# Modulation as columns and as broadcast rows on the chip, without a trip through DRAM, in a long two-block kernel

## The chip, the cores and the metric

One core of one Trainium2 chip. The metric is the device time of one execution in microseconds, the median of several runs. Everything is float32; the large matrix products use a split of each operand into a high and a low fp32r half and three products of them, and the small ones plain f32.

## The reference, cut to what matters

256 tokens of width 1024 go through two layers of a first block and two of a second. Only the first block has the modulation, a vector of 6 x 1024 numbers for each layer:

```python
c_act = jax.nn.silu(c)                                   # (1, 1024)
for layer in range(2):
    mod = c_act @ mod_w[layer] + mod_b[layer]            # (1, 6144)
    sh_m, sc_m, gt_m, sh_f, sc_f, gt_f = jnp.split(mod[:, None, :], 6, axis=-1)
    h = x * (1 + sc_m) + sh_m
    u, q, k, v, g_out, a_low = jnp.split(h @ w_in[layer], IN_SPLITS, axis=-1)
    y = concat([s5(u), gla(q, k, v, g_out, a_low)]) @ w_out[layer]
    x = layer_norm(ALPHA * x + (1 + gt_m) * y, ...)
    h = x * (1 + sc_f) + sh_f
    f = swiglu(h) if layer % 2 == 0 else moe(h)
    x = layer_norm(ALPHA * x + (1 + gt_f) * f, ...)
```

Shifts and scales (sh, sc) are used with features on partitions, so the kernel wants them as columns (128 partitions, 8 numbers each). The gates (gt) multiply a result with tokens on partitions, so they are wanted as rows that stand on all 128 partitions.

## The kernel before

Each engine has its own program, written as strands (generators) that a function `weave` runs piece by piece in the order of a string in `ORDERS`, one string for each stage and engine. A letter is one piece; a piece reaches to the next `yield`. An engine executes strictly in that order, so a piece that waits holds up all behind it. Between stages stands a `fence` of all engines. SP issues all large weight loads in one order, 1 MB each (128 partitions x 2048), into a ring of five slots `RG`; a slot is loaded again when its user has said so (`W.raw_used` for those used as they are).

`mod_w` has 12 blocks of 512 columns for each layer, two loads each. `plan_mod` plans blocks 0 to 3 of layer 0 (shift and scale of the mixers) ahead of `w_in`, blocks 4 to 11 in the mixers of layer 0, and blocks 6 to 9 of layer 1 in the mixers of layer 1. What layer 1 needs otherwise comes from sums made beside the feed-forward; these don't change here, apart from the row sums' place in the order.

- `pe_mod`: one column of c (`sm(24 + k, 1)`, 128x1) is the stationary operand, 512 columns of the weight stream past it; 8 matmuls for a block give one row on one partition, in bank 3. The trace shows each f32 matmul as two records.
- `a_mod`: ACT copies the row (1x512) to SBUF and issues its DMA to `mod_rows` in DRAM. The next block waits for the copy.
- `a_cols`, `pe_cols`, `v_cols`: when all rows are in DRAM, a DMA reads them back with 128 numbers in a line, TensorE transposes them, and VectorE adds the bias `MB` and 1.
- `a_gate`, `v_gate`: the gates of layer 0 are read back from DRAM onto all partitions, the bias beside them into `ROWT`; VectorE adds both and 1 (128x1024, twice for each gate). Both gates share `ROWT`.

The strands of the stage "start" are `p` (`pe_first`, `v_first`, `a_first`: small transposes of biases and gains, the four blocks, the columns, then the scaled and transposed input `h_mod` in four quarters and the projection `w_in` in 17 parts) and `r` (the S5 coefficients: row arithmetic on 32 partitions, their transposes to `PC`, the input matrices in four rounds `v_s5_in`, then jobs B, C and K on TensorE, each emptied by ACT or VectorE). The stages "mixers0" and "mixers1" have strands `s` (S5: products of 32 rows and 64 columns, a long block of VectorE operations on 128x1024 with two scans, then products back), `g` (gated linear attention: decay, key transposes and the copy of keys `KD`, states, six levels of decayed queries and keys, scores, outputs), `m` (`pe_mods`, `v_mods`, `a_mods`) and `b` (VectorE: S5 weights of layer 1; ACT: loads for later). Small loads go out on ACT's queue, each as an instruction of its own in ACT's order.

Of the kernel before, what the change touches and what calls it, by code (L numbers as in the profile page):

```python
# [8 lines left out]
F32 = mybir.dt.float32  # L9
# [325 lines left out]
def weave(eng, stage, **strands):  # L335
# [37 lines left out]
def build(nc, w):  # L373
    ctx = ExitStack()
    with ctx:
# [44 lines left out]
        mrow = nc.dram_tensor("mod_rows", (2, 6144), F32, kind="Internal").ap()  # L420
# [35 lines left out]
        ROWT = ROWS[:, 2560:3584]  # L456
        g2 = lambda n, l: w[n + "_2"][l]
# [93 lines left out]
        c_in, first_in = signal("c_in", by=16), signal("first_in", by=16)  # L551
        silu_v, silu_a = signal("silu_v"), signal("silu_a")
        mod_pe, mod_a = signal("mod_row_pe"), signal("mod_row_a")
        row_sent = [signal(f"mod_row_sent{i}", by=16) for i in range(4)]
        cols_in, cols_pe, cols_v = signal("mod_cols_in", by=16), signal("mod_cols_pe"), signal("mod_cols_v")
        gate_in, gate_v = signal("gate_rows_in", by=16), signal("gate_rows_v")
# [7 lines left out]
        def mod_index(l, n):  # L564
            return n if l == 0 else 6 + n

        def pe_mod(pe, l, n):
            i = mod_index(l, n)
            pe.wait_ge(silu_v, 0, "c")
            pe.wait_ge(mod_a, i)  # L570
            pe.wait_ge(cols_v, (i >= 4) + (i >= 12))
            for ld in W.of["mod", l, n]:
                if ld.g:
                    yield
                pe.wait_ge(W.landed[ld.slot], ld.use)
                for k in range(4):
                    x = pe.mm(PS[0:1, 3, :], sm(24 + ld.g + k, 1), ld.dst[:, k, :], ld.g + k == 0, ld.g + k == 7)
                x.then_inc(W.raw_used)
            yield

        def a_mod(a, l, n):
            i = mod_index(l, n)
            ld = W.of["mod", l, n][1]
            row = ROWT[0:1, n % 2 * 512:(n % 2 + 1) * 512] if l else MOD[0:1, (n % 4) * 512:(n % 4 + 1) * 512]
            a.wait_ge(*ld.raw)
            if l == 0:
                a.wait_ge(row_sent[n % 4], i // 4)
            elif n >= 8:
                a.wait_ge(row_sent[(n - 2) % 4], 4)
            a.act(row, PS[0:1, 3, :], ACT.Copy).then_inc(mod_a)  # L590
            a.dma(mrow[l:l + 1, n * 512:(n + 1) * 512], row).then_inc(row_sent[n % 4])


        COLS = ((0, 0, 4, 4), (0, 6, 10, 12), (1, 6, 10, 16))

        def a_cols(a, k):
            l, n0, n1, sent = COLS[k]
            for r in range(4):
                a.wait_ge(row_sent[r], sent // 4)
            if k:  # L600
                a.wait_ge(cols_pe, k)
# [18 lines left out]
        def a_gate(a, i, dst):  # L620
            k = int(i == 5)
            for r in range(4):
                a.wait_ge(row_sent[r], 3)
# [2687 lines left out]
```

## Time and profile before

| | us |
|---|---|
| three runs | 2982.76, 2988.92, 2990.46 (median 2988.92) |
| the execution that was profiled | 2986.9 |
| its span, first to last instruction | 2985.1 |
| TensorE busy | 2556.5 (86%) |
| VectorE busy | 2058.9 (69%) |
| ScalarE busy | 1566.1 (52%) |
| mean granted TensorE clock | 0.905 of 2.4 GHz |

The stages follow each other by fences: the start to 133 us, the mixers of layer 0 to 289, output and feed-forward to 634, the projection of layer 1 to 694, its mixers to about 831, then the mixture of experts and the second block. In a timeline a line is one instruction or a run of like ones ("x16"), with start, length, and in brackets how long the engine had been idle before it and what released it. PE is TensorE, PEld its weight loads, DVE VectorE, ACT ScalarE; a q behind the name is the engine's queue of DMA issues or semaphore work. The length of a matmul record holds its way through the array, so the pace of a run is read from the starts. "fp32r" and f32 weights are both listed as f32.

### The profile page before, as it was taken

The numbers are of one execution on the slowest core, as the hardware profiler recorded it, in microseconds if no ns is written. First come the engines' busy times: TensorE is split into PE (matmuls) and PEld (weight loads), VectorE is DVE, ScalarE is ACT, GpSimd is POOL, SyncE is SP. The second block draws the span as 40 slices with busy tenths as digits, with TensorE's granted clock in tenths as the row PEclk, the third lists the DMA queues.
The fourth block names the chain that finished last, engine by engine and source line by source line (L and its number), as shares of the span: only waits on it lengthen the run. The fifth ranks groups of instructions, "written<-read, shape, count | busy, mean of one in ns | idle before, by whom it ended". The sixth has DMA issues, their size and how long they took to land.

```text
span 2985.1 us, 31552 instructions
## 1 busy us (share of the span) xinstructions
PE 2556.5 (86%) x11718; PEld 1997.7 (67%) x11718; DVE 2058.9 (69%) x2204; ACT 1566.1 (52%) x1938; POOL 24.4 (1%) x33
## 2 busy tenths in 40 slices
PE   5997789977967999999999999968686998786898
PEld 2736677855556777777777777756455786555787
DVE  5597786755666888887978888874664554565454
ACT  2222434432146878787787878753533544543443
POOL 0000000000100000000000000000000000000000
PEclk9987999986978999999999999988777999877899
DMA  8461367731335998898989898974012454303352
GB/s 254 129 195 38 108 215 263 272 114 49 111 116 195 328 330 326 310 349 303 345 320 355 327 333 331 339 258 142 23 57 85 156 188 145 113 24 104 100 186 96
DMA packets 274723, 599.15 MB, mean 201 GB/s; under 512 B 28801, under 2 KB 35311, under 8 KB 273409
## 3 DMA queue, kind: packets, MB, share of 16 engines
q1 hardware_dynamic: 252144, 580.30, 54.8%
q10 hardware_dynamic: 22418, 16.77, 2.1%
q8 instruction: 94, 1.54, 0.2%
q14 instruction: 67, 0.55, 0.1%
HBM read 595.93 MB, written 1.09 MB: 200 GB/s over the span
## 4 chain that ended last, share of the span: by engine, by line
PE 61%; DVE 23%; ACT 10%; issue 2%; ACTq 1%; DMA 1%; DVEq 0%; POOL 0%; POOLq 0%; PEldq 0%
PE PS L205 59%; DVE WL L167 8%; ACT WH L197 3%; PE PS L213 2%; ACT AR L197 2%; DVE AR L167 2%; DVE MW L167 2%; ACTq L146 1%; DVE WF L167 1%; ACT MW L197 1%; DVE HF L167 1%; DVE MOD L167 1%; ACT L197 1%; ACT WF L197 1%; DVE HTR L167 1%
## 5 line engine op out<-in xcount | busy, mean ns | idle before, releaser
L167 DVE TENSOR_TENSOR WL<-RG,WH 128x1024 fp32r<-128x1024 f32 (+1 forms) x558 | 919.4, 1648 | 446.7 <-ACT WH L197 417.6
L197 ACT ACTIVATE WH<-RG 128x1024 fp32r<-128x1024 f32 x782 | 827.4, 1058 | 594.1 <-PE PS L205 527.6
L205 PE MATMUL PS<-WH,HTR 128*128 128x512 f32 (+3 forms) x2920 | 926.2, 393 | 63.2 <-DVE HTR L167 21.9
L205 PEld LDWEIGHTS PS<-WH,HTR 128*128 128x128 f32 x2920 | 557.7, 194 | 197.7 <-DVE WL L167 40.4
L205 PE MATMUL PS<-WL,HTR 128*128 128x512 f32 (+3 forms) x1460 | 569.1, 390 | 0.0
L205 PE MATMUL PS<-WH,ATR 128*128 128x512 f32 x1624 | 522.5, 395 | 16.6 <-DVE WL L167 9.3
L205 PEld LDWEIGHTS PS<-WH,ATR 128*128 128x128 f32 x1624 | 309.2, 190 | 85.0 <-DVE WL L167 19.1
L205 PE MATMUL PS<-MW,HTR 128*128 128x512 f32 x1332 | 330.0, 397 | 18.1 <-DVE MW L167 18.1
L205 PE MATMUL PS<-WL,ATR 128*128 128x512 f32 x812 | 319.8, 394 | 0.0
L205 PEld LDWEIGHTS PS<-WL,HTR 128*128 128x128 f32 x1460 | 282.7, 194 | 52.5
L167 DVE TENSOR_TENSOR MW<-RG,MW 128x2048 fp32r<-128x2048 f32 x112 | 256.7, 2292 | 64.1 <-ACT MW L197 53.4
L205 PEld LDWEIGHTS PS<-MW,HTR 128*128 128x128 f32 x1332 | 248.3, 190 | 70.7 <-DVE MW L167 20.3
L197 ACT ACTIVATE MW<-RG 128x1024 fp32r<-128x1024 f32 x224 | 237.9, 1062 | 25.2 <-PE PS L205 2.5
L205 PEld LDWEIGHTS PS<-WL,ATR 128*128 128x128 f32 x812 | 154.8, 191 | 31.5
L213 PE MATMUL PS<-KC,AR 128*128 128x128 f32 (+2 forms) x716 | 118.1, 301 | 63.0 <-DVE AR L167 24.3
L213 PEld LDWEIGHTS PS<-KC,AR 128*128 128x128 f32 (+2 forms) x716 | 94.2, 156 | 90.0 <-DVE AR L167 30.8
L205 PE MATMUL PS<-RG,SMALL 128*1 128x512 f32 x256 | 121.2, 625 | 9.1 <-ACT ROWS L197 5.2
L197 ACT ACTIVATE AR<-PS,SMALL 128x128 f32<-128x128 f32 (+3 forms) x146 | 77.5, 531 | 75.8 <-PE PS L205 67.9
L197 ACT ACTIVATE AR<-PS 128x512 f32<-128x512 f32 (+3 forms) x120 | 66.7, 556 | 82.2 <-PE PS L205 50.0
L213 PE MATMUL PS<-KC,X 128*128 128x128 f32 x160 | 33.8, 393 | 81.1 <-ACTq L155 31.1
L197 ACT ACTIVATE ATR<-PS 128x512 fp32r<-128x512 f32 x102 | 61.1, 599 | 80.3 <-PE PS L213 75.4
L213 PEld LDWEIGHTS PS<-KC,X 128*128 128x128 f32 x160 | 29.3, 207 | 85.5 <-DVEq L155 37.3
(219 smaller groups left out, 2037.7 us busy)
## 6 DMA issues: line engine op xcount, KB each, us to landing
RG<-in_moe_w_gate SPq DMA_DIRECT2D x112, 1024.0 KB, 5.7
RG<-in_moe_w_up SPq DMA_DIRECT2D x112, 1024.0 KB, 5.8
RG<-in_moe_w_down SPq DMA_DIRECT2D x112, 1024.0 KB, 6.2
RG<-in_w_ff SPq DMA_DIRECT2D x64, 1024.0 KB, 5.2
RG<-in_mod_w SPq DMA_DIRECT2D x48, 1024.0 KB, 5.3
RG<-in_w_in SPq DMA_DIRECT2D x36, 1024.0 KB, 5.2
RG<-in_w_out SPq DMA_DIRECT2D x16, 1024.0 KB, 5.0
RG<-in_ffn_w_gate SPq DMA_DIRECT2D x14, 1024.0 KB, 5.2
```

The source lines that it names most:

```text
L146: return Ins(self.e.dma_start(dst, src, **kw) if self.e is not None else None, self)
L167: return self.did(lambda: self.e.tensor_tensor(o, a, b, op))
L197: return self.did(lambda: self.e.activation(o, a, f, bias=bias, scale=scale))
L205: return self.did(lambda: self.e.matmul(o, l, r, start=start, stop=stop))
L213: return self.did(lambda: self.e.transpose(o, a, perm))
```

## The change

The row on one partition, its copy to DRAM and its reading back are gone. Blocks that are needed as columns (0 to 3 and 6 to 9) hold 128x128 pieces of the weight as the stationary operand and stream one column of c past them: 16 matmuls of one column for a load, 128 for the eight loads of four blocks, into 32 columns of bank 3 (16 for each half of the sum); VectorE adds the two halves and the bias. Blocks that are needed as rows (4, 5, 10, 11 of layer 0) hold c on all 128 columns (`CBC`, 8 pieces of 128x128 made once by VectorE in `ROWT`), so that the result stands on all partitions; VectorE adds it and 1 to the bias, which has been loaded into the gate's place. ACT has no part in it any more. TensorE waits for the constants as its first act. The loads for S5 (`a_s5_in(a, 0)`) are issued after ACT's row pieces and no more before the first stage; the small transposes of biases come after the four blocks. The orders of the start and of both mixers are others.

```diff
 ORDERS = {
-    ("mixers0", "a"): "gmsbmsbgmgsggmmmmmggggggmsmmsggggsgggsmssggg",
+    ("mixers0", "a"): "gsbmsbggsggsgggsgggsgggssggsggggg",
-    ("mixers0", "pe"): "mmggsmmsmmmmsmmgsmmgmggmggmsmssggssssggsssggsssggsssgsmssssggggggggg",
-    ("mixers0", "v"): "bggsbgsgbgsmgssssgbbggbggbggbgggggggggsggggggsgggggmgmsggmggsggssgggggg",
+    ("mixers0", "pe"): "mmmgmsmgsmmmmmmmmgsssssssgmggssssgsgmsssssssggsmggsggsggmgsggggggggg",
+    ("mixers0", "v"): "mgsbmbgsmggbgsssssgbgbgmgggbggsgggggggsgmbgsgbgggggmggsgggsgsgggggggggggg",
-    ("mixers1", "a"): "sgmbssggggsgggsgggsgggbggmgsgssmmggmmg",
+    ("mixers1", "a"): "gsmbbgssgggsggggggsgggggggssssggg",
-    ("mixers1", "pe"): "sggsmmgsssgsgsggsgsmssssssssssssggmsggmsgmgggsgmsmggmgmgggmggmgmm",
-    ("mixers1", "v"): "gsbmsgggsgggssssggmgggggggggggmgssgmsgmggggggggggsgssgggggggggggmg",
+    ("mixers1", "pe"): "ggsmmmsmgsssgmggsmsggmsmssssggssssgssgsggsggsgmmssggmggmgssgggmgm",
+    ("mixers1", "v"): "bgsmgggsmgmsggssssggmggmggggggggggsggsgggggggggggsggggggsgssggmggg",
-    ("start", "a"): "rprrrpppprrrprppprprrrpppppppppppppppppppppp",
-    ("start", "pe"): "ppprpppprpprrrrrppppprrrrrrrrrpppppppppppppppppp",
-    ("start", "v"): "rpprrrrrrrrrrrrprrprprpprpprppprrppppppppppppppppppppp",
+    ("start", "a"): "rprrrrpprrrpprrrpppppprrpppppppppppppppp",
+    ("start", "pe"): "prppppprpppprrrrrpppprppprrppppppppppprrprrprprp",
+    ("start", "v"): "rprrrrrrrrrrrppppppppppprpprrppppppppppppppppprrrrrprp",
...
+        CBC = ROWT.rearrange("p (k n) -> p k n", k=8)
...
+        MODS = (0, 0, 4), (0, 4, 1), (0, 5, 1), (0, 6, 4), (0, 10, 1), (0, 11, 1), (1, 6, 4)
+
+        def pe_mod(pe, i):
+            l, n0, m = MODS[i]
             pe.wait_ge(silu_v, 0, "c")
+            for n in range(n0, n0 + m):
+                for ld in W.of["mod", l, n]:
+                    yield
+                    if n == n0 and ld.g == 0:
+                        pe.wait_ge(mod_v, i)
+                    pe.wait_ge(W.landed[ld.slot], ld.use)
+                    if m == 1:
+                        for k in range(4):
+                            x = pe.mm(PS[:, 3, :], CBC[:, ld.g + k, :], ld.dst[:, k, :], ld.g + k == 0, ld.g + k == 7)
+                    else:
+                        for j in range(4):
+                            c = ld.g * 4 + (n - n0) * 4 + j
+                            for k in range(4):
+                                x = pe.mm(PS[:, 3, c:c + 1], ld.dst[:, k, j * 128:(j + 1) * 128], sm(24 + ld.g + k, 1),
+                                          k == 0, k == 3)
+                    x.then_inc(W.raw_used)
+
+        def v_mod(v, i):
+            l, n0, m = MODS[i]
+            v.wait_ge(*W.of["mod", l, n0 + m - 1][1].raw)
+            if m == 1:
+                dst = (GTM if n0 < 6 else GTF)[:, n0 % 2 * 512:n0 % 2 * 512 + 512]
+                v.wait_ge(gate_in, 2)
+                v.stt(dst, PS[:, 3, :], 1.0, dst, ADD, ADD).then_inc(mod_v)
+                return
+            a_ = 48 * l + 4 * n0
+            v.tt(MC[:, a_:a_ + 16], PS[:, 3, 0:16], MB[:, a_:a_ + 16], ADD)
+            v.tt(MC[:, a_:a_ + 16], MC[:, a_:a_ + 16], PS[:, 3, 16:32], ADD).then_inc(mod_v)
+            v.ts(MC[:, a_ + 8:a_ + 16], MC[:, a_ + 8:a_ + 16], 1.0, None, ADD)
+
+        def a_gate_bias(a):
+            for i, dst in ((2, GTM), (5, GTF)):
+                a.dma(dst, rowb(w["mod_b"][0, i * 1024:(i + 1) * 1024])).then_inc(gate_in)
...
         def pe_first(pe):
-            yield
-            pe.wait_ge(first_in, 7)
+            yield from pe_mod(pe, 0)
+            yield
+            pe.wait_ge(first_in, 6)
             pe.tr(PS[:, 7, 0:96], CB[0:96, 128:256], KC[0:96, K_ID:K_ID + 96])
             pe.tr(PS[:, 7, 96:144], CB[0:48, 256:384], KC[0:48, K_ID:K_ID + 48]).then_inc(pro_pe)
-            for n in range(4):
-                yield from pe_mod(pe, 0, n)
-            pe_cols(pe, 0)
             yield
             pe.wait_ge(pro_v, 1)
+            pe.wait_ge(mod_v, 1)
             yield from pe_w_in(pe, 0)
...
         def a_s5_first(a):
             yield from a_s5_rows(a)
+            yield
+            a_s5_in(a, 0)
             yield from a_s5_jobs(a, 0, S5_BANKS[0], JOBS)
 
         def pe_program(pe):
+            pe.wait_ge(consts_in, 1)
...
             v.tt(sm(24, 8), CB[:, 0:8], sm(16, 8), MUL).then_inc(silu_v, "c")
+            v.wait_ge(consts_in, 1)
+            for k in range(8):
+                v.ts(CBC[:, k, :], KC[:, K_ONE:K_ONE + 128], sm(24 + k, 1), None, MUL)
```

## Rows read from the trace of the kernel before

**Rows 1.** The page, chain that ended last, shares by engine.
```profile
PE 61%; DVE 23%; ACT 10%; issue 2%; ACTq 1%; DMA 1%; DVEq 0%; POOL 0%; POOLq 0%; PEldq 0%
```

**Rows 2.** Windows: stretch, length, busy PE, PEld, DVE, ACT, POOL, clock, DMA, GB/s.
```profile
82.00:133.00 51.00, 50.85 (x240) 43.19 (x239) 23.11 (x29) 16.20 (x19) 0.00 (x0) 0.96 0.39 125
133.00:289.00 156.00, 132.58 (x703) 72.80 (x703) 131.28 (x202) 32.23 (x50) 8.87 (x12) 0.80 0.40 125
694.00:835.00 141.00, 102.72 (x656) 63.63 (x656) 92.83 (x140) 33.06 (x49) 9.35 (x12) 0.77 0.21 68
755.00:822.00 67.00, 60.07 (x276) 30.79 (x275) 43.23 (x59) 9.91 (x19) 5.49 (x7) 0.97 0.39 127
```

**Rows 3.** Timeline of the start: start, length, engine, operation, count, idle before.
```profile
19.50 8.57 PE L205 MATMUL PS<-RG,SMALL 128*1 128x512 f32 x16
...
29.54 7.03 PE L205 MATMUL PS<-RG,SMALL 128*1 128x512 f32 x16 [1.47 <-ACT MOD L197]
...
46.12 0.43 DVE L167 TENSOR_TENSOR MOD<-MOD,PC 128x256 f32<-128x256 f32 x1
...
50.32 0.42 DVE L167 TENSOR_TENSOR MOD<-MOD,PC 128x256 f32<-128x256 f32 x1
...
53.03 0.22 ACTq L146 DMA_DIRECT2D mod_rows<-MOD  x1
...
71.12 10.31 PE L205 MATMUL PS<-AR 128*128 128x128 f32 x64 [2.15 <-DVE AR L171]
...
75.70 2.36 DVE L172 TENSOR_SCALAR H<-PS,SMALL 128x256 f32<-128x256 f32 x4
...
81.74 0.50 PE L205 MATMUL PS<-WH,HTR 128*128 128x512 f32 x1
```

**Rows 4.** Timeline, TensorE, feed-forward of layer 0: one-column products.
```profile
502.10 3.63 PE L205 MATMUL PS<-SMALL,H 128*128 128x1 f32 x32
```

**Rows 5.** Windows, columns as in group 2: narrow blocks.
```profile
128.40:133.00 4.60, 4.45 (x22) 4.36 (x21) 0.11 (x1) 0.11 (x1) 0.00 (x0) 0.51 0.00 0
502.00:505.60 3.60, 3.60 (x35) 3.56 (x33) 1.23 (x1) 1.06 (x1) 0.00 (x0) 1.00 0.25 100
```

**Rows 6.** Timeline, TensorE, last block of the first projection: 16 columns.
```profile
125.76 0.26 PE L205 MATMUL PS<-WL,HTR 128*128 128x16 f32 x1
...
126.10 0.26 PE L205 MATMUL PS<-WL,HTR 128*128 128x16 f32 x1
...
129.72 0.36 PE L205 MATMUL PS<-WL,HTR 128*128 128x16 f32 x1
...
130.36 0.36 PE L205 MATMUL PS<-WL,HTR 128*128 128x16 f32 x1
```

**Rows 7.** Timeline, mixers of layer 0: TensorE, then VectorE.
```profile
154.95 13.24 PE L205 MATMUL PS<-H,AR 32*128 32x64 f32 x256 [1.75 <-DVE H L181]
...
171.26 2.47 DVE L167 TENSOR_TENSOR HF<-AR,PS 128x1024 f32<-128x1024 f32 x2
...
191.07 0.69 DVE L167 TENSOR_TENSOR WF<-WF 128x512 f32<-128x512 f32 x1
...
200.36 0.69 DVE L181 COPY WF<-PS 128x512 f32<-128x512 f32 x1
...
214.35 10.10 DVE L167 TENSOR_TENSOR WF<-WF 128x128 f32<-128x128 f32 x18
...
263.47 1.22 DVE L167 TENSOR_TENSOR MOD<-MOD,ROWS 128x1024 f32<-128x1024 f32 x1 [0.93 <-DMA ROWS<-in_mod_b]
```

**Rows 8.** Timeline, mixers of layer 1: ACT, VectorE, TensorE.
```profile
786.33 0.95 ACT L197 ACTIVATE WF<-WF 128x256 f32<-128x256 f32 x2 [6.38 <-issue]
...
786.78 4.28 DVE L167 TENSOR_TENSOR WF<-WF 128x256 f32<-128x256 f32 x7 [4.12 <-ACT WF L197]
...
788.01 4.88 PE L205 MATMUL PS<-RG,SMALL 128*1 128x512 f32 x8 [5.19 <-ACT ROWS L197]
...
828.44 0.28 PE L213 MATMUL PS<-KC,ST 16*128 16x16 f32 x1 [6.76 <-DMA ST<-mod_rows]
```

More of the change, by code:

```diff
@@ L360 @@
     ("attention1", "v"): "kbccddddbbcbccdckddkbcdbcdbccddccbdbdcdcbcdbcccdbdddddcbcddcdbcbckkk",
-    ("start", "a"): "rprrrpppprrrprppprprrrpppppppppppppppppppppp",
-    ("start", "pe"): "ppprpppprpprrrrrppppprrrrrrrrrpppppppppppppppppp",
-    ("start", "v"): "rpprrrrrrrrrrrrprrprprpprpprppprrppppppppppppppppppppp",
+    ("start", "a"): "rprrrrpprrrpprrrpppppprrpppppppppppppppp",
+    ("start", "pe"): "prppppprpppprrrrrpppprppprrppppppppppprrprprrprp",
+    ("start", "v"): "rprrrrrrrrrrrppppppppppprpprrppppppppppppppppprrrrrprp",
     ("out0", "a"): "xxrrwwrxxrrwwwrrwxrrxxwwwwwxwxwwwxxxxxxxx",
@@ L549, in build @@
         oown = {x: signal("over_own_" + x) for x in ("v", "a", "g")}
-        c_in, first_in = signal("c_in", by=16), signal("first_in", by=16)
+        c_in, consts_in, first_in = signal("c_in", by=16), signal("consts_in", by=16), signal("first_in", by=16)
         silu_v, silu_a = signal("silu_v"), signal("silu_a")
[L553 to L556, printed above, removed]
+        mod_v, gate_in = signal("mod_v"), signal("gate_bias_in", by=16)
         rows_in = signal("rows_in", by=16)
@@ L574, in pe_mod @@
                     yield
[L575 to L578, printed above, removed]
-            yield
[L581 to L591, printed above, removed]
@@ L594, in build @@
[L594 to L601, printed above, removed]
-            m = 4 * (n1 - n0)
-            a.dma(ST[0:m, 384:512], mrow[l, n0 * 512:n1 * 512].rearrange("(j p) -> j p", p=128)).then_inc(cols_in)
-        def pe_cols(pe, k):
-            l, n0, n1, sent = COLS[k]
-            m = 4 * (n1 - n0)
-            pe.wait_ge(cols_in, k + 1)
-            pe.wait_ge(mod_a, sent)
-            pe.tr(PS[:, 3, 0:m], ST[0:m, 384:512], KC[0:m, K_ID:K_ID + m]).then_inc(cols_pe)
@@ L612, in v_cols @@
-        def v_cols(v, k):
-            l, n0, n1, sent = COLS[k]
-            a_, b_ = 48 * l + 4 * n0, 48 * l + 4 * n1
-            v.wait_ge(cols_pe, k + 1)
-            v.tt(MC[:, a_:b_], PS[:, 3, 0:b_ - a_], MB[:, a_:b_], ADD)
-            c = 48 * l + 8 * (1 if n0 == 0 else 4)
-            v.ts(MC[:, c:c + 8], MC[:, c:c + 8], 1.0, None, ADD).then_inc(cols_v)
[L620 to L623, printed above, removed]
-            a.wait_ge(gate_v, k)
-            a.dma(dst, rowb(mrow[0, i * 1024:(i + 1) * 1024])).then_inc(gate_in)
-            a.dma(ROWT, rowb(w["mod_b"][0, i * 1024:(i + 1) * 1024])).then_inc(gate_in)
@@ L1456, in pe_mods @@
                 pe.wait_ge(sums_v, 0, "row3")
-            for n in (range(6, 10) if l else range(4, 12)):
-                yield from pe_mod(pe, l, n)
-            pe_cols(pe, 1 + l)
+                yield from pe_mod(pe, 6)
+            else:
+                for i in range(1, 6):
+                    yield from pe_mod(pe, i)
         def v_mods(v, l):
@@ L1463, in v_mods @@
                 yield from v_row_sums(v)
-            yield
-            v_cols(v, 1 + l)
-            v_ln_cols(v, l, 8 * l, 16 + 8 * l, 4)
-            if l == 0:
+            for i in ((6,) if l else range(1, 6)):
                 yield
-                v_gate(v, 2, GTM)
-                yield
-                v_gate(v, 5, GTF)
-        def a_mods(a, l):
-            for n in (range(6, 10) if l else range(4, 12)):
-                yield
-                a_mod(a, l, n)
-            yield
-            a_cols(a, 1 + l)
-            if l == 0:
-                yield
-                a_gate(a, 2, GTM)
-                yield
-                a_gate(a, 5, GTF)
+                v_mod(v, i)
+                if i in (3, 6):
+                    v_ln_cols(v, l, 8 * l, 16 + 8 * l, 4)
         def nothing(*_):
@@ L1503, in a_mixers @@
         def a_mixers(a, l):
-            weave(a, f"mixers{l}", s=a_s5(a, l), g=a_gla(a, l), m=a_mods(a, l),
+            weave(a, f"mixers{l}", s=a_s5(a, l), g=a_gla(a, l), m=iter(()),
                   b=once(lambda: (a_second_in(a), a_ln_rows(a, 1, "mix", 1))) if l else once(lambda: a_s5_in(a, 1)))
@@ L3054, in a_first @@
         def a_first(a):
-            for n in range(4):
-                yield
-                a_mod(a, 0, n)
-            yield
-            a_cols(a, 0)
             for _ in range(4):
```

20 lines of the change are left out of this document (3 added, 17 removed).

## The prediction

> **What bounds the kernel now.** I read the shares of the chain first, then the busy time by stage, then the timelines of the three stages that the change touches. TensorE has most of the chain, VectorE the next share [rows 1]. The change works in the start (0 to 133 us), in the mixers of layer 0 (133 to 289) and of layer 1 (694 to 835). The projection inside the start keeps TensorE busy for all of its 51 us; in the first mixers VectorE (131 of 156 us) and TensorE (133) are both nearly full; in the second TensorE has 103 and VectorE 93 of 141 [rows 2]. So in the start and late in both mixers a TensorE microsecond is a microsecond of the kernel; under the long VectorE block of the recurrence it is free.
>
> In the start TensorE does nothing until 19.5 us, because its first piece waits for the last small load; then come four row products (first records at 19.50, a later group 7.03 us for 16 records), the last row leaves for DRAM at 53.03, the scaled input is formed at 75.70, and the projection starts at 81.74 [rows 3].
>
> **Cost of the new product.** Before, one 1 MB load is 4 matmuls of 512 columns, 8 records. As columns it is 16 matmuls of one column, each behind a 128x128 f32 weight load, 32 records. The trace holds this very shape once: 32 records in 3.63 us, the last start 3.4 us behind the first, so 0.108 us a record and 3.45 us a load at the 2.4 GHz level [rows 4]; its window shows a granted clock of 1.00 [rows 5]. That equals the row form (half of 7.03, [rows 3]): at full clock the change of form is free.
>
> At the lower level it isn't. The last block of the projection is the nearest long run of narrow matmuls: 16 columns, weights of 128 columns loaded back to back. It begins at full clock with 3 records in 0.34 us; some 3 us later 3 records take 0.64 us, 0.213 each [rows 6], and the window shows 0.51 although TensorE is busy for 4.45 of 4.60 us [rows 5]. So a TensorE that loads weights all the time and streams next to no columns falls to 1.2 GHz, and a weight-load-bound record doubles. One column is further that way than 16. The burst of [rows 4] lasted 3.6 us between wide matmuls and says nothing of 28 us. Ends for one load: 3.45 us and 32 x 0.213 = 6.8 us. I take 6.8 for the runs of eight loads, since the 16-column row is the nearest long one, and a value between for scattered loads. The Trainium skill (page "TensorE: Matmul & The Clock Gate", LDWEIGHTS) prices a weight load at its columns over 1.2 GHz, with no word of the granted clock. By it the load would stay near 3.4 us; the rows at 0.110 and 0.213 us disagree.
>
> **Start.** Removed: four ACT copies, four writes to DRAM, the read back, one transpose, and the wait of the first product for the small loads. Added: a wait for the constants (issued first) and eight 128x128 VectorE operations, about 2 us before VectorE's first row piece, which waits for its own loads anyway: 0. Gate bias loads and the S5 loads move on ACT's queue; they end well before their users: 0 to +1, as the first scaled copy stands behind seven issues instead of five.
> - TensorE starts at about 9 us, an estimate: it needs c and the first MB, which is moved beside the constants; the first window of the trace has no row for either. Five loads at 6.8: 43. Row transposes 2: 45. Three loads: 65.5. Small transposes 1, five S5 jobs at 0.9 to 1.7: 74.
> - VectorE: PC copy, then three rounds of the S5 input at 4.2 us (46.12 to 50.32 [rows 3]): 59, no bound. Bias and modulation: 67. Then four low halves, the last held by ACT's S5 copies and high halves: 76, then scaling, which took 6.0 us to the first matmul (75.70 to 81.74): 82 to 83. So the projection starts 1 us later than before, though the DRAM trip is gone.
> - The new order also puts S5 jobs inside the projection: three B jobs, two C jobs (5 x 0.87, from 8 records at 0.108) and the four K jobs, before at 71.12 in 10.31 us, partly at low clock [rows 3], at 0.108 for 64 records 6.9. That is 11 us on a TensorE that has none free there.
> Sum +12. At full clock: five loads end by 29, VectorE's rows at 32 and its three rounds bind instead (51), projection at 62, plus 62: 124, so -9.
>
> **Mixers of layer 0.** Two row loads, two more, then S5's 32-row products (13.24 us, [rows 7]), as before. Then TensorE has eight column loads in one string, the key transposes behind them. From the stage start: 34 + 8 x 6.8 = 88.5, transposes to 90. VectorE does its block (19.8 us from 171.26 to 191.07), two S5 rounds, and wants the keys at about 65; before it got them at 200.36, 67.4 us into the stage [rows 7]. It stands idle until 90: +22.5. Behind that the order has seven S5 pieces, the state products and a row load before VectorE's levels, which before began at 214.35, 81.3 us in; now about 109, as the pieces were under the wait before: +28. Off come two gate pieces on VectorE (1.2 + 0.7 each) and a wait of 0.93 for a DMA [rows 7]; on come four adds of 128x512 (0.7, as the copy of that size) and one S5 round that has moved late: 0. Sum +28. At full clock the string ends at 62, under VectorE's 65, and the stage gains 2.
>
> **Mixers of layer 1.** Gains: the read back through DRAM at the end (TensorE waited 6.76 us; about 4 of it are on the path, because ACT's table load and VectorE's last product stand behind it), and ACT's 13 issues in mid-stage, for which VectorE stood 4.12 us and TensorE 5.19 [rows 8]. These issues now come as ACT's first work of the stage, 6.3 us, ahead of the gate's exponentials and the copy that S5's products wait for: +4. Column loads are scattered among 31 us of other TensorE work (60 busy from 755 to 822, [rows 2], less 29 for the loads). If all eight ran at the low level it would be +27, none 0; I take half, 13, because each load alone is as short as the burst that kept its clock, while pairs aren't. Sum 13 + 4 - 4 - 4 = +9; bounds -4 and +23. ACT's eleven other row copies were never late: 0.
>
> **Sum.** 12 + 28 + 9 = +49 us on the execution that was profiled, 2986.9 (span 2985.1), which is 2.0 below the median 2988.92: 3036. Weights for the later stages use the same ring of five slots, and their stages are untouched: 0.
>
> **Rivals.**
> 1. *Weight loads keep their pace* (clock stays at 2.4 GHz, or the load doesn't follow it). For: the one-column burst held 1.00 [rows 5]. Against: the 16-column run. Then start -9, first mixers -2, second -4: 2972, faster.
> 2. *The low clock comes, but where TensorE has room.* For: the second block of idle TensorE under the recurrence is some 20 us long. Against: in the start and in the first mixers the string is longer than its cover. If the string in the first mixers cost only 5, and the second mixers nothing: 2986.9 + 12 + 5 - 1 = 3003; with a start at 0 it is 2991.
> 3. *The low clock spreads*: full-duty work behind each scattered load also starts low, as TensorE does after the row 128.40 to 133 [rows 5]; second mixers at +23, start at +20: 3058.
> 4. *The change doesn't do what it says*, the DRAM trip was hidden anyway: the start and the tail of the second mixers gain nothing even at full clock. Then the moved S5 jobs alone count, between 0 and +11: 2990 to 3000. It decides only if rival 1's clock holds.
>
> Rival 1 takes over where a column load costs less than about 4.4 us: each microsecond above 3.45 is worth 6 in the start (21 over 3.35) and 4 in the second mixers, and 8 in the first mixers from 3.8 us on, where their string outgrows its cover; with these, -15 becomes 0 at 4.4.
>
> **How the numbers follow.** Forecast with its own spread (3015 to 3050) 0.55; rival 3 0.15; rival 1 0.18; rivals 2 and 4 together 0.12. The time is that of the likeliest, 3036. The range leaves out little of the first two and reaches down to rival 1: 2970 to 3060, 0.9 of the chance less the tails, some 0.8; the likeliest's own is 3015 to 3050. A measurement of this kernel tells about 0.3%, 9 us, from no change. Faster by more: 0.19 (rival 1 and a little of 4). Within: 0.06. Slower: 0.75.
>
> **What the new profile would show.** Right: records of one column 0.213 us apart over nearly all of 9 to 65 us, granted clock 0.5 there; in the first mixers a string of 256 such records over 54 us and VectorE idle over 20 us before the key copy; projection beginning at 82 and lasting 62. Wrong: one-column records at 0.108 us through a whole string, or a projection that begins before 70. The step most open is the clock under one-column products longer than 3.6 us; the second is how many of the scattered loads fall low. If TensorE starts later than 12 us, the loads and not the clock bind the start.

## The result, and the profile after

The changed kernel takes 3061.8 us (median; 3057.5 to 3082.8), the kernel before 2989.4 in the same session: ratio 1.026 (95% interval 1.023 to 1.028), some 72 us slower. The profiled execution took 3063.1 us, 3061.3 of it span. The forecast was 3036, its range ended at 3060.

I cut both traces at the same five events: the projection's first matmul, ScalarE's copy of its last 16 columns, the first matmul that waits for GpSimd at the end of the first mixers, the same copy in layer 1, and the same matmul at the end of the second mixers. Each stage is the time between two of them, in us, one profiled execution each (a difference of two rounded times can be off by 0.1):

```
                         before    after   difference   forecast
start to projection        81.7     81.1      -0.6         +1
projection                 51.2     61.0      +9.9        +11
mixers of layer 0         156.2    185.4     +29.2        +28
middle of the layer       405.1    409.6      +4.5          0
mixers of layer 1         137.6    169.9     +32.3         +9
rest                     2153.3   2154.2      +0.9          0
span                     2985.1   3061.3     +76.2        +49
```

The timeline of the changed kernel, TensorE in the start and in the first mixers, then VectorE's copy of the keys (start, length, engine, line, operation, count, idle before it and what ended that), to be read against [rows 3] and [rows 7]:

```profile
9.80 34.27 PE L205 MATMUL PS<-SMALL,RG 128*128 128x1 f32 x160 [9.80 <-DMA RG<-in_mod_w]
...
45.41 20.64 PE L205 MATMUL PS<-SMALL,RG 128*128 128x1 f32 x96
...
176.35 54.77 PE L205 MATMUL PS<-SMALL,RG 128*128 128x1 f32 x256
...
232.11 0.69 DVE L181 COPY WF<-PS 128x512 f32<-128x512 f32 x1 [22.12 <-PE PS L213]
```

The records are 0.214 us apart from 9.8 to 66 us (34.27 over 160) and again for 54.77 us in the first mixers, where one short burst in the kernel before had 0.113 [rows 4]. VectorE stands idle for 22.12 us before the keys. It copies them 89.9 us into the stage, 22.4 later than before; the forecast had 90 and 22.5. Windows of the changed kernel (stretch, length, busy PE, PEld, DVE, ACT, POOL, clock, DMA, GB/s), against [rows 2] and [rows 5]:

```profile
8.00:66.00 58.00, 56.20 (x269) 56.15 (x269) 31.01 (x90) 4.52 (x7) 0.00 (x0) 1.00 0.75 235
176.00:231.00 55.00, 55.00 (x265) 54.88 (x262) 31.75 (x43) 5.97 (x7) 0.00 (x0) 0.50 0.42 134
737.00:907.00 170.00, 142.90 (x839) 126.68 (x839) 91.78 (x139) 27.62 (x42) 8.88 (x12) 0.58 0.18 57
```

The string of the first mixers runs at the lower level (0.50 is 1.2 GHz) although TensorE is busy for 55.00 of 55.00 us. The clock was at that level before the string began, at 165 us, under S5's 32-row products; it didn't come back until the string was over. In the start the clock column says 1.00 at the very same pace of records; there the pace is what counts (last section).

In the second mixers nearly all loads ran low, and so did much of what stands between them. TensorE there, late in the stage:

```profile
847.06 3.35 PE L205 MATMUL PS<-WF 64*128 64x128 f32 x14
850.34 6.98 PE L205 MATMUL PS<-SMALL,RG 128*128 128x1 f32 x32
857.25 3.35 PE L205 MATMUL PS<-WF 64*128 64x128 f32 x14
860.53 0.79 PE L205 MATMUL PS<-AR,WF 128*128 128x128 f32 x2
861.26 0.79 PE L205 MATMUL PS<-WF 64*128 64x128 f32 x2
861.98 6.98 PE L205 MATMUL PS<-SMALL,RG 128*128 128x1 f32 x32
```

Six loads take 6.98 or 6.99 us each. The two that stand together (from 831.38) take 11.32, because they begin at full clock and lose it on the way (last section). The same fourteen score matmuls (64 rows, 128 columns) that take 1.82 us at full clock take 3.35. The windows from 845 to 890 us, between and under the loads alike, show 0.50 and a TensorE without a gap:

```profile
845.00:860.00 15.00, 15.00 (x67) 14.46 (x67) 4.03 (x5) 0.22 (x1) 0.00 (x0) 0.50 0.25 80
860.00:875.00 15.00, 15.00 (x64) 14.01 (x64) 5.57 (x6) 0.00 (x0) 0.00 (x0) 0.50 0.33 120
875.00:890.00 15.00, 15.00 (x64) 13.87 (x63) 5.68 (x8) 1.86 (x3) 0.00 (x0) 0.50 0.00 0
```

In the kernel before, the window from 755 to 822 us had 0.97 [rows 2].

### The profile page after: what moved, and what is told of

Same layout as the page of the kernel before. It is cut to its first block, busy times and chain, and to the rows that moved or that the text cites. A ratio compares the mean times of both kernels' runs of the same rounds, so it can differ in the third digit from the quotient of the medians.

```text
span 3061.3 us, 32653 instructions
## 1 busy us (share of the span) xinstructions
PE 2654.5 (87%) x12291; PEld 2174.0 (71%) x12291; DVE 2059.2 (67%) x2215; ACT 1556.7 (51%) x1922; POOL 24.0 (1%) x33
## 4 chain that ended last, share of the span: by engine, by line
PE 66%; DVE 20%; ACT 9%; issue 2%; DMA 1%; ACTq 1%; DVEq 0%; POOL 0%; SPq 0%; POOLq 0%; PEldq 0%
PE PS L205 63%; DVE WL L167 7%; PE PS L213 3%; ACT WH L197 3%; ACT AR L197 2%; DVE MW L167 2%; DVE AR L167 1%; ACT MW L197 1%; DVE MOD L167 1%; ACT L197 1%; DVE HTR L167 1%; DVE WF L167 1%; ACT WF L197 1%; DVE H L167 1%; DVE X L167 1%
## 5 line engine op out<-in xcount | busy, mean ns | idle before, releaser
L205 PE MATMUL PS<-SMALL,RG 128*128 128x1 f32 x768 | 162.9, 349 | 9.8 <-DMA RG<-in_mod_w 9.8
L205 PEld LDWEIGHTS PS<-SMALL,RG 128*128 128x128 f32 x768 | 162.1, 328 | 12.0 <-issue 11.6
L213 PE MATMUL PS<-KC,X 128*128 128x128 f32 x160 | 32.5, 387 | 80.3 <-ACTq L155 30.6
```

The lines of the kernel that those rows point to most:

```text
L205: return self.did(lambda: self.e.matmul(o, l, r, start=start, stop=stop))
L213: return self.did(lambda: self.e.transpose(o, a, perm))
```

## The experiments

**The theory.** A long run of one-column products pulls TensorE to 1.2 GHz or holds it there, and the whole loss comes from that. Rivals: the column form itself costs it at any clock; the new orders and waits cost it; ScalarE's small-load issues at the head of the second mixers cost 4 us, as the prediction had it.

**1. The same products, 128 equal columns wide.** The moving operand is the same column of c read 128 times. Other widths weren't tried. Weight loads, order and waits stay; only what TensorE streams behind each load grows. The last product to write a column of PSUM is the one meant for it, and the second half of the sum lies from column 256 on, where VectorE reads it.

```
-c = ld.g * 4 + (n - n0) * 4 + j
+c = ld.g * 64 + (n - n0) * 4 + j
-x = pe.mm(PS[:, 3, c:c + 1], ld.dst[:, k, ...], sm(24 + ld.g + k, 1), ...)
+x = pe.mm(PS[:, 3, c:c + 128], ld.dst[:, k, ...], sm(24 + ld.g + k, 1).broadcast_to([128, 128]), ...)
```

> Changed kernel, but every column product streams 128 equal columns of c instead of one (same weight loads, same number of matmuls; one of the 128 result columns is used). Clock theory: the one-column strings are slow because TensorE falls to 1.2 GHz; with 128 columns it stays at 2.4 and a record takes 0.108 us instead of 0.213. Then the start is some 9 us shorter than in the kernel before (projection from about 62 us), the mixers of layer 0 about 154 us long instead of 185, those of layer 1 about 134 to 140 instead of 170: near 2970 us in all, faster than the kernel before. Shape theory (a one-column product with weights from the ring costs 0.21 us whatever the clock; more columns can't make it cheaper): stays at 3060 or above. Order theory (the new orders cost most of it): records at 0.108 but stages still long, 3020 to 3050.

Measured: 2992.2 us, ratio to the kernel before 1.001 (0.9997 to 1.002). So 70 of the 72 us go, with as many instructions as in the changed kernel and 128 times the columns. TensorE's timeline, start and first mixers:

```profile
9.69 20.69 PE L206 MATMUL PS<-SMALL,RG 128*128 128x128 f32 x160 [9.69 <-DMA RG<-in_mod_w]
...
168.18 30.72 PE L206 MATMUL PS<-SMALL,RG 128*128 128x128 f32 x256
```

The first string takes 20.69 us instead of 34.27, the second 30.72 instead of 54.77. Windows inside the second string, its first records and the rest:

```profile
168.10:172.00 3.90, 3.90 (x22) 3.83 (x19) 3.21 (x7) 3.78 (x4) 0.00 (x0) 0.50 0.00 0
173.00:199.00 26.00, 26.00 (x235) 26.00 (x235) 24.80 (x30) 0.85 (x2) 0.00 (x0) 1.00 0.84 270
```

This is the plainest evidence for the clock: one string of equal products, 0.213 us a record while the window shows 0.50 and 0.112 us while it shows 1.00. The string begins at the lower level, as in the changed kernel; with 128 columns the clock rises inside it, with one it never did. The window over the second mixers, against 0.58 and 142.90 busy above:

```profile
704.00:838.00 134.00, 107.70 (x843) 91.57 (x843) 91.93 (x139) 27.87 (x43) 8.88 (x12) 0.75 0.23 72
```

That stage takes 133.2 us, 36.7 less than in the changed kernel. TensorE's busy time shrinks by 35.2. Grouped by operation over the stage (count | busy us, mean ns | idle), the changed kernel first:

```profile
L205 PE MATMUL PS<-SMALL,RG 128*128 128x1 f32 x256 | 53.2, 343 | 0.0
L205 PE MATMUL PS<-WF 64*128 64x128 f32 x136 | 26.8, 359 | 0.0
```

and with 128 columns:

```profile
L206 PE MATMUL PS<-SMALL,RG 128*128 128x128 f32 x256 | 32.0, 284 | 0.0
L206 PE MATMUL PS<-WF 64*128 64x128 f32 x136 | 19.1, 283 | 0.3 <-DVE WF L168 0.3
```

The column products themselves account for 21.2 us of the 35.2, the scores for 7.7 and the other short matmuls for 6.3: two fifths of the loss in this stage lie in work that the change doesn't touch. The form rival falls. So does the order rival as the main cause, since the orders are the changed kernel's; what they cost by themselves stands below, under the mixers of layer 0.

The time was expected near 2970 us and is 22 above. The first mixers took 158.9 us (154 expected) and the middle 411.5 (405.1 before). The largest miss is the start: the projection began at 72.9 us, not at 62. VectorE's and ScalarE's timelines show why:

```profile
16.91 6.54 ACTq L147 DMA_DIRECT2D MOD<-in_s_b_im  x1
23.48 12.51 ACTq L147 DMA_DIRECT2D MOD<-in_s_c_re  x1
...
48.40 0.42 DVE L168 TENSOR_TENSOR MOD<-MOD,PC 128x256 f32<-128x256 f32 x1 [14.75 <-DMA SMALL<-in_s_b_glu]
```

The change moved the S5 loads behind ScalarE's exponentials. ScalarE is at issuing them until 40.94, and VectorE waits 14.75 us for the last. In the changed kernel VectorE stood 13.13 us for the row transposes behind the slow string instead, which hid this.

**2. ScalarE's issues later in the second mixers.** They are 15; the prediction and the expectation call them 13, the rows of the timeline, two of which are pairs. On top of the last kernel:

```
-("mixers1", "a"): "gsmbbgssgggsggggggsgggggggssssggg"
+("mixers1", "a"): "gsmbgssgggbsggggggsgggggggssssggg"
```

> As wide128, and ACT's 13 small-load issues of the mixers of layer 1 put behind the last exponential ahead of VectorE's long block, where ACT idled for some 30 us in the changed kernel, instead of first in the stage. If they delay the copy that S5's products wait for, as I reckoned at +4, this is 4 to 6 us faster than wide128; if the path there went by TensorE or VectorE anyway, the same.

Measured: 2994.1 us, ratio to the kernel before 1.001 (0.9997 to 1.002); the stage took 132.9 instead of 133.2 us. The issues cost nothing where the change put them.

**3. 128 columns in the second mixers alone.** The width is 128 for layer 1 and 1 elsewhere.

> The changed kernel with 128 equal columns in the eight loads of the second layer alone; those of the start and of the first layer keep their one column. Theory (each stage loses by its own low clock, and nothing carries over): start 142 us and the first mixers 185 us as in the changed kernel, the second mixers 133 us as in the wide one instead of 169.9, so 3022 to 3028 us. Rival (the clock lost in the first layer is paid in the second too, or a change of the order there is part of the loss): the second mixers at 140 to 165 us, 3030 to 3055 us.

Measured: 3028.0 us, ratio 1.012 (1.009 to 1.015). Start 142.3 and first mixers 182.8 us, near the changed kernel's 142.2 and 185.4; second mixers 136.9. The stage is 33 us shorter than in the changed kernel, about half of the 70 us that the clock costs in all, and the start and the first mixers keep their own loss. The 136.9 lies between the 133 of the theory and the 140 of the rival, but run 6, whose code is run 1's in this stage, read 136.7 there, so it is within the spread of the stage. Stages don't pay for each other, as far as that spread tells.

**4. The eight loads of the second mixers in one string, one column wide.**

```
-("mixers1", "pe"): "ggsmmmsmgsssgmggsmsggmsmssssggssssgssgsggsggsgmmssggmggmgssgggmgm"
+("mixers1", "pe"): "ggsmmmsmgsssgmggsmsggsssssggssssgssgsggsggsgmmmmmmmmssgggggssgggg"
```

> The changed kernel, one column as it has it, with the eight loads' products of the second layer together in one string instead of scattered in six places over the stage. Theory (a scattered piece pulls its neighbours down: of the 36 us that the low clock costs in this stage, some 21 lie in the column products themselves and some 14 in the short matmuls between them): the string runs low as a whole, 52 to 56 us for 256 records, but the others get the full clock back, and the stage takes 156 to 163 us instead of 169.9, so 3048 to 3055 us. Rival (all of the loss goes with the column products, wherever they stand): the stage stays at 168 to 172 us and the time at 3060 to 3064. Third case (the string waits for its loads, or keeps the others waiting, and this costs more than the clock gives back): over 172 us.

Measured: 3077.9 us, ratio 1.029 (1.027 to 1.032): the stage took 186.6 us, 16.7 more than scattered. The first expectation is refuted. TensorE around and behind the string:

```profile
820.97 0.71 PE L205 MATMUL PS<-WF 64*128 64x128 f32 x4
821.61 51.95 PE L205 MATMUL PS<-SMALL,RG 128*128 128x1 f32 x256
873.49 1.96 PE L205 MATMUL PS<-KC,HF 63*128 63x63 f32 x8
875.38 2.61 PE L205 MATMUL PS<-H,MOD 128*128 128x256 f32 x8
877.92 3.35 PE L205 MATMUL PS<-WF 64*128 64x128 f32 x14
```

and the window behind it, where nothing of one column is left:

```profile
875.00:915.00 40.00, 28.63 (x111) 25.23 (x110) 21.20 (x33) 5.83 (x8) 0.00 (x0) 0.50 0.07 26
```

A window inside the string shows the fall without a gap in TensorE's work:

```profile
822.00:870.00 48.00, 48.00 (x238) 48.00 (x239) 7.95 (x14) 2.82 (x7) 4.54 (x6) 0.53 0.44 144
```

TensorE enters the string fast, comes out at 1.2 GHz and stays there to the end of the stage, with the ordinary short matmuls alone.

**5. The same one string, 128 columns wide**, as the control for run 4.

> The order with one string in the second mixers, with 128 equal columns: the control for that run, where the stage took 186.6 us. Theory (the string lost its time by the clock: TensorE came out of it at half clock and stayed there to the end of the stage): 133 to 139 us in this stage, as in the scattered order with 128 columns. Rival (the order itself costs it, the other work waits behind the string): 148 to 155 us, some 17 above the scattered order, as in the narrow pair (186.6 against 169.9).

Measured: one execution, 3016.7 us; the stage took 157.9 us, 24.7 more than the scattered order at the same width. The rival is the nearer one: the order itself costs it, as the rest of the stage waits behind the string. TensorE:

```profile
791.91 28.85 PE L206 MATMUL PS<-SMALL,RG 128*128 128x128 f32 x256
...
823.07 1.82 PE L206 MATMUL PS<-WF 64*128 64x128 f32 x14
...
829.48 3.35 PE L206 MATMUL PS<-WF 64*128 64x128 f32 x14 [0.49 <-DVE MOD L168]
```

```profile
829.00:850.00 21.00, 17.63 (x68) 15.62 (x68) 10.44 (x12) 1.92 (x4) 0.00 (x0) 0.50 0.00 0
```

Here the string runs at full clock, and the same scores cost 1.82 us behind it, but 3.35 from 829 on: late in this stage TensorE falls to the lower level with no one-column product in it. So run 4 doesn't show that the narrow string alone holds the clock down to the end; between the two strings 28.7 us are the clock's, 23.1 of them in the string.

**6. The sums in the middle, widened too.** In the middle the kernel before already has sixteen one-column products (32 records). They took 3.63 us there [rows 4] and 4.78 in the changed kernel, and wide matmuls behind them ran slow.

```
-x = pe.mm(PS[:, 5, j:j + 1], HROW[:, j * 128:(j + 1) * 128], COL[:, 1:2], True, True)
+x = pe.mm(PS[:, 5, j:j + 128], HROW[:, j * 128:(j + 1) * 128], COL[:, 1:2].broadcast_to([128, 128]), True, True)
```

> The kernel with 128 equal columns, and the sixteen one-column sums in the middle of the layer (32 records) widened in the same way to 128 equal columns. Theory (the 3 to 4 us that the middle of the layer loses comes from the granted clock falling at this short string of one-column matmuls): the 32 records take 3.6 to 3.9 us instead of 4.67, the clock stays at 1.00 behind them, and the middle takes 407 to 409 us instead of 411.5, so 2988 to 2990 us. Rival (the middle is longer for another reason, and the short string only happens to lie there): the middle stays at 411 to 412 and the time at 2992 us.

Measured: 2990.0 us, ratio 0.999 (0.998 to 1.0005), against 1.001 without: the difference is inside the intervals. The stage took 406.8 us instead of 411.5, and the 32 records 3.73 us; the second mixers, unchanged in the code, took 136.7 instead of 133.2, so the whole shows little of it. The profiles of the other kernels agree: where the narrow burst took 3.63 us (before, before with early loads, run 4) the middle is 405.1 to 406.2 us long; in the seven others it took 4.65 to 4.87 and the middle 409.3 to 411.6. But both kernels without the change were on the short side, and seven of eight with it on the long one. Whether the change itself tips the burst or not was tried with a small shift: one or two more clears of a 128x1024 tile (0.91 us each) on VectorE at the head of this stage, in both kernels.

```
-for at in (HROW, GTM, ROWT):
+for at in (HROW, GTM, ROWT) + (GTM,):          # or + (GTM, GTM)
```

> The kernel before with one more clear of a 128x1024 tile on VectorE at the head of the feed-forward of layer 0, so that the sixteen one-column sums (32 records) come about 1 us later. Theory (these sums fall low or not by when they come, and the change only moved them in time): of the four shifted kernels some take 3.6 us for the records and some 4.6 to 4.9, in both families, and the middle is 405 to 407 us, or 409 to 412, with it, plus the shift of up to 1 us. Rival (something that the change does to the stage drops the clock there): both shifted kernels of the family before take 3.63 us and 405 to 407 us.

> The same with two more clears, about 2 us later. Same theories: a mixture over the four, or 3.63 us here and middle 405 to 408.

> The changed kernel with one more clear at the same place. Theory (time alone decides): a mixture over the four kernels, 3.6 or 4.6 to 4.9 us for the 32 records, middle 405 to 408 or 409 to 412. Rival (the change does it): 4.6 to 4.9 us and 409 to 412 here.

> The changed kernel with two more clears. Same theories as for one: a mixture over the four, or 4.6 to 4.9 us here.

Measured, one execution each: burst and middle in us are 3.63 and 408.4, then 3.81 and 411.9 for the kernel before with one and two clears, and 3.63 and 405.8, then 3.88 and 410.0 for the changed kernel. Windows from the start of the burst on, the kernel before with two clears first, then the changed kernel with one:

```profile
507.60:511.40 3.80, 3.80 (x34) 3.80 (x32) 1.23 (x1) 1.06 (x1) 0.00 (x0) 0.93 0.22 91
511.40:516.00 4.60, 4.60 (x16) 3.69 (x16) 0.00 (x0) 0.31 (x1) 0.00 (x0) 0.69 0.67 230
```

```profile
538.60:542.20 3.60, 3.60 (x34) 3.58 (x33) 1.23 (x1) 1.06 (x1) 0.00 (x0) 1.00 0.25 102
542.20:547.00 4.80, 4.80 (x22) 3.94 (x22) 0.73 (x1) 1.06 (x1) 0.00 (x0) 1.00 0.67 220
```

With a shift, the clock falls in the kernel before as well, and holds in the changed one, whose time (3052.7 us in that execution) is lower with a clear more than without. So both families know both outcomes, and the rival (something that the change does in the stage) falls.

What decides is open. The shifts weren't the ones intended: the burst begins 213.0 us into the stage in the kernel before and at 216.3 and 218.2 with one and two clears, but at 214.2 in the changed kernel and at 213.6 and 216.3 with them. And each kernel was profiled once, so that a difference between executions of one kernel isn't told from one between kernels. What the burst is worth is plainer when counted from its first record to the end of the stage: 192.1 or 192.2 us where the clock holds, 193.7 where it falls as the burst ends (both kernels with two clears, and run 4), and 195.3 to 196.8 where it falls inside the burst.

**7. The S5 loads of layer 0 from GpSimd's queue**, on top of the 128 columns. GpSimd has nothing to do in the start. Each of the four large loads is cut in two halves, on a semaphore of their own.

```
-            a_s5_in(a, 0)          # ScalarE, behind its exponentials
+            a_s5_in(g, 0)          # GpSimd, first of all
```

> The kernel with 128 equal columns, and the S5 loads of the first layer issued from GpSimd's queue, which is idle there, ahead of everything (each of the four large ones in two halves). In the wide kernel VectorE stands for 14.75 us, until 48.40, for the last of these loads, because ScalarE issues them from 16.47 to 40.94 us. Theory (the S5 loads' late issue on ScalarE is what holds the start): the wait is gone or under 3 us, the projection begins at 62 to 65 us instead of 73.0, everything behind moves up by as much, 2981 to 2984 us, some 6 to 9 us below the kernel before. Rival (the transfers themselves fill the DMA engines until about 48 us, whoever issues them): VectorE waits as long as before, projection at 71 to 75, 2990 to 2994 us.

Measured: 2985.4 us, ratio 0.997 (0.996 to 0.998). The projection begins at 65.4 us instead of 72.9.

```profile
40.89 0.43 DVE L168 TENSOR_TENSOR MOD<-MOD,PC 128x256 f32<-128x256 f32 x1 [6.71 <-DMA SMALL<-in_s_b_glu]
```

VectorE still waits 6.71 us, for the last small load. The issue was what held the start, though not all of it.

**8. The same edit in the changed kernel, one column wide, and in the kernel before.**

> The changed kernel with its one-column products, and the S5 loads from GpSimd's queue alone. Theory (with one column the start is bound by TensorE's string, which lasts until 66 us and hides ScalarE's issuing): the projection begins at 80 to 82 us as in the changed kernel, end of the start 141 to 143, so the S5 loads are worth 0 here, where they are worth 7.6 behind the wide products. Rival (they cost in both): projection at 73 to 77.

> The kernel before the change with the one edit that the S5 loads of the first layer are issued from GpSimd's queue. Theory (the start before the change is bound by the chain of four rows to DRAM and back, which the profile shows to end at 71.1 us, and the S5 loads lie beside it): projection still at 79 to 82, time 2987 to 2991 us, so the gain of 7 us needs the change's way without the trip. Rival (ScalarE's 14 us of issuing also holds the four rows' evictions, so the chain moves up with it): projection at 74 to 78, 2981 to 2985 us, and the change would be worth nothing in itself.

Measured: one execution of the changed kernel, 3063.6 us, projection at 82.1 and end of the start at 143.2 (142.2 without): no gain. The kernel before: 2991.2 us, ratio 0.999 (0.998 to 1.000), projection at 83.4 (81.7 without). Neither gains, as the theories had it (the projection of the second is 1.7 us later, which they hadn't). The late S5 loads cost nothing behind a slow string or behind the trip to DRAM, and 7.5 us behind fast products.

**9. The three edits together, then VectorE waiting for the B loads alone.** `best` joins 128 columns, wide sums and GpSimd's loads; `best2` adds to it:

```
-v.wait_ge(s5_soft_in, 10)     # all S5 loads, before the first block work
+v.wait_ge(s5_b_in, 4)         # B alone
+v.wait_ge(s5_c_in, 6)         # C, skip and gate bias: before the C matrix
```

> Three edits together on the changed kernel: 128 equal columns for the column products, the same for the sixteen sums in the middle of the layer, and the first layer's S5 loads from GpSimd's queue. Theory (the three gains lie in different stages and add): start 126.5 us to the end of the projection, first mixers 158.5, middle 405 to 407 instead of 409 to 411, second mixers 133 to 136, 2980 to 2983 us, ratio 0.996 to 0.998 to the kernel before. Rival (the middle's gain was the luck of one execution): 2985 us, as with the S5 loads alone.

> As the last, and VectorE's first block work waits for the B loads alone, on a semaphore of their own; the C loads, the skip and the gate bias are waited for only where the C matrix is formed. With the S5 loads on GpSimd, VectorE still stood 6.71 us, to 40.89, for the last small load, while GpSimd had issued the B halves by 24.9. Theory: that wait ends by 35 to 37, the projection begins at 60 to 62 instead of 65.4, and the time is 2976 to 2979 us. Rival (something else is the last before the projection: the w_in weights' conversion, X's transposes): the projection stays at 64 to 66 and the time at 2980 to 2983.

Measured: 2978.8 us, ratio 0.9955 (0.9943 to 0.9968), then 2970.8, ratio 0.9925 (0.9912 to 0.9938). Both intervals lie below 1, so both beat the kernel before. The first time lies just under its expectation, as it should if the gains of runs 6 and 7 add to run 1, though run 6's alone was inside its intervals. In the last, VectorE and TensorE:

```profile
32.97 0.56 DVE L182 COPY PC<-PS 128x384 f32<-128x384 f32 x1 [1.04 <-PE PS L214]
33.63 0.43 DVE L168 TENSOR_TENSOR MOD<-MOD,PC 128x256 f32<-128x256 f32 x1
...
59.70 0.79 PE L206 MATMUL PS<-WH,HTR 128*128 128x512 f32 x1 [9.88 <-DVE HTR L168]
```

There is no wait left between the two VectorE lines, and the projection begins at 59.7 us, 22 earlier than in the kernel before. By stage against the kernel before: start 120.9 (-12.0), first mixers 157.9 (+1.7), middle 405.6 (+0.5), second mixers 133.7 (-3.9), which is -13.7. The rest read 2147.6 us (-5.8); it is the same code in all kernels and read 2148.5 to 2156.2 in the sixteen other profiles, so most of that part looks like the spread of the stage. The time lies 5 us under the expected 2976; no run tells whether that is the spread too.

## Why the prediction failed, step by step

- **One-column products at half clock (right).** The weighing of the 16-column rows [rows 6] against the short burst [rows 4] came out as taken: 0.214 us a record, 6.8 to 7.0 us a load. Run 1 shows that it is the clock and not the load: with 128 columns behind every weight load, records are 0.213 us apart at 0.50 and 0.112 at 1.00, in one string. The Trainium skill (page "TensorE: Matmul & The Clock Gate", section LDWEIGHTS) prices a load by its columns alone, which makes 0.107 us for 128 of them, an estimate by that page. The records at full clock agree with it, those at the lower level are twice as far apart.
- **Start, +12 (right, +9.3).** The string began at 9.8 us (forecast about 9) and the projection at 81.1 (forecast 82 to 83), then lasted 61.0 (forecast 62).
- **S5 loads on ScalarE's queue at no cost (right by its number, wrong by its reason).** The text said that they end well before their users. They ended when VectorE was still held by TensorE's transposes (13.13 us). With fast products it waited 14.75 us for them. So rival 1's start was wrong too: 134.1 us, where it forecast 124. It would have missed by 10 us in this term.
- **Mixers of layer 0, +28 (right in the string, and in the sum by some luck, +29.2).** The string outgrew its cover as reckoned: the keys came 22.4 us later, forecast 22.5. The levels behind them began 105.6 us into the stage, 24.1 later than before, where 28 was forecast. The small terms behind them were put at 0. By the prediction's own prices they come to +2.3 (an S5 round of 4.2 and four adds of 0.7, less 4.7), and from the levels to its end the stage took 79.7 us instead of 74.8. Two errors of some 4 to 5 us cancel. The second is there at either width: the thirteen profiles with the new order have 77.0 to 80.3 us behind the levels, the four with the old 74.8 to 75.1. So at full clock (run 1) the levels began 2.8 us earlier than before and the stage was still 2.7 longer, where the prediction had a gain of 2. How the 2 to 5 us divide between the S5 round and two row loads that now stand there on TensorE (6.42 and 3.70 us in run 1) no run tells. Five other profiles with the same code in this stage read 182.3 to 182.9 us, so +29.2 is the upper end of +26 to +29.
- **Mixers of layer 1, +9 with bounds -4 and +23 (wrong, +32.3).** This is the step that failed, and with it the sum. It had three faults. First, it took half of the eight loads as low "because each load alone is as short as the burst that kept its clock"; all but the head of one pair were (six of 6.99 us, two in 11.32). The two at 795 and 803 us began at 0.50, and the pair lost the clock, with all behind it. Why these loads ran low where the burst kept its clock isn't shown. The surroundings differ: the burst stood between wide matmuls, these loads among short ones, which in run 5 ran low from 829 us on with no one-column product about. Secondly, its upper bound priced the loads alone. The neighbours lost 14.0 us more. Thirdly, its small terms were off but cancelled: ScalarE's issues at the head cost nothing clear of the spread (0.3 in run 2), not 4, and the two gains of 4 came to less than 5 together, as the stage is 4.4 us shorter than before at full clock. By the runs the term is +21.2 for the loads (13 was taken), +14.0 for their neighbours and +1.5 of idle time (none was), and -4.4, which is the +32.3.
- **Middle, 0 (wrong by size, +4.5).** The prediction called the middle untouched. The one-column burst there holds the full clock or loses it, in either family of kernels (run 6): from its first record on the stage is 3.3 us longer than before. The prediction had its row in hand [rows 4] and should have put these microseconds into the range. The other 1.3 us lie ahead of the burst and aren't traced.
- **Rivals.** Rival 3, the low clock that spreads to the work behind, named the mechanism of the failed term, at too small a size (+23 for that stage) and with a start of +20 that didn't come. Rival 1's ends show in run 1 for the second mixers (-4.4, it said -4). Against rival 4 speaks run 7 beside the kernel before with the same early loads: the start ends at 126.5 us instead of 135.3. So the start gains by the change at full clock. How much of it is the trip to DRAM and how much TensorE's earlier first product (11.1 instead of 22.1 us in these two) no run separates. In rival 2 the gain of 1 us in the second mixers has no source; by the prediction's own terms for that stage it would be 4. That makes 3000 of its 3003 and bears on no chance.

## What to carry to other kernels

A matmul with one moving column is not cheap because it streams little: price it at the lower clock, price the short matmuls around it at the lower clock too, and only then ask what hides it. In the stage that the prediction missed, the loads cost 21.2 us more and their neighbours 14.0. If its weight loads bind anyway, try the same products with equal columns added to the moving operand; here 128 of them, the one width tried, cost no instruction and gave 70 us back. When a slow step is made fast, look again at every transfer that it had hidden, since a cost that was called nothing is often only covered.

## What was not expected of the hardware

- TensorE busy for 55.00 of 55.00 us stayed at a granted clock of 0.50 (first mixers of the changed kernel), and the same 256 products with 128 columns took 30.72 us and rose to 1.00 within them. In run 4 the clock fell from 1.00 under one-column products, with TensorE busy for 48.00 of 48.00 us. The Trainium skill (page "TensorE: Matmul & The Clock Gate", "HAM oscillation — how this bites in real kernels") puts the fall of the clock down to idle gaps; the rows here have none.
- From a stretch at 1.00 (826 to 831 us in the changed kernel) the clock fell within two loads of one column:

```profile
831.40:833.50 2.10, 2.10 (x20) 2.10 (x20) 0.99 (x3) 1.43 (x3) 0.76 (x1) 1.00 0.01 4
835.00:838.00 3.00, 3.00 (x16) 3.00 (x15) 2.76 (x6) 0.54 (x2) 1.46 (x2) 0.50 0.30 33
```

- In the start the clock column reads 1.00 from 8 to 66 us while the records are 0.214 us apart, the pace of the windows that read 0.50. The trace's first clock record stands at 69.6 us, and ahead of it the column prints 1.00 for want of one. With 128 columns (run 1) the first record is a rise at 15.1 us, and there the products go from 0.213 us to 0.112. The same page of the Trainium skill ("Seeing it yourself") warns that these events aren't always reliable; here the pace of equal records was the safe reading for 56 us.
- The issues of six loads, four of them of 128 KB, kept ScalarE's queue for 24.5 us (16.47 to 40.94) beside the weight stream, single issues for 6.54 and 12.51 us; in the changed kernel the same issues took 16.0 us (16.80 to 32.84). The ten issues ahead of them took 0.28 to 0.58 us each. So an issue has no fixed price. The four large loads come in 2048 pieces of 64 bytes or 512 of 256 each, and no run separates that from the weight stream beside them.
